# Filler matmuls, projections of rows not yet normed, and the recurrence's preparation woven into attention

## What is computed

```python
u = rmsnorm(h, attn_norm_pre[l])
proj = u @ w_in[l]
o_fox = forgetting_attention(fh(fq), fh(fk), fh(fv), ff, fox_forget_bias[l])   # 8 heads of 64, causal softmax
o_rwkv = rwkv7_time_mix(p_rwkv, ...)    # 8 heads of 64, a recurrence over the tokens
mix = jnp.concatenate([o_fox, o_rwkv], axis=-1) @ w_out[l]

# rwkv7_time_mix:
p_prev = jnp.concatenate([jnp.zeros_like(p[:, :1]), p[:, :-1]], axis=1)
p = p + shift_mu * (p_prev - p)
w = -jax.nn.softplus(-(w0 + jnp.tanh(w_lat) @ w_up)) - 0.5
a = jax.nn.sigmoid(a0 + a_lat @ a_up)
g = jax.nn.sigmoid(g_lat) @ g_up
kk = kk / jnp.maximum(jnp.linalg.norm(kk, axis=-1, keepdims=True), 1e-12)
S_t = S diag(w_t) + (S a_t) b_t^T + v_t k_t^T ;  y_t = S_t r_t
```

## Time and profile before

| | us |
|---|---|
| median of 3 runs | 3685.21 |
| lowest, highest | 3672.19, 3711.24 |
| profiled execution, own time | 3717.66 |
| its span | 3715.6 |
| PE busy | 3496.1 (94%) |
| DVE busy | 1811.7 (49%) |
| ACT busy | 1259.8 (34%) |
| POOL busy | 809.1 (22%) |
| mean granted clock | 0.955 |

### The profile page before, as it was taken

The page is one execution under the profiler, slowest core; times in us unless marked ns, Lnnn a source line. Parts: engine busy times, 40 slices in busy tenths (PEclk is TensorE's granted clock), DMA queues, the critical chain, the costliest instruction groups (busy, mean ns, idle before and its releaser), DMA issues.

```text
span 3715.6 us, 47117 instructions
## 1 busy us (share of the span) xinstructions
PE 3496.1 (94%) x16820; PEld 2843.6 (77%) x16820; DVE 1811.7 (49%) x3443; ACT 1259.8 (34%) x1663; POOL 809.1 (22%) x336
## 2 busy tenths in 40 slices
PE   7995999799997889999899999999999899999998
PEld 5662897568785777888787888888888788888886
DVE  2554441343204554222312489998989254444443
ACT  2223210233224553333323343344444233332332
POOL 5430000234442333333444434400000000000000
PEclk9996985899998999999999999999999999999999
DMA  3110000122232122222222334445555655555642
GB/s 115 52 46 6 1 1 1 46 74 96 86 101 69 67 68 74 74 72 70 79 96 91 106 117 142 140 156 178 193 179 178 223 201 187 186 193 206 204 147 75
DMA packets 145965, 408.07 MB, mean 110 GB/s; under 512 B 11176, under 2 KB 43944, under 8 KB 143536
## 3 DMA queue, kind: packets, MB, share of 16 engines
q1 hardware_dynamic: 73472, 265.85, 22.3%
q10 hardware_dynamic: 72368, 140.68, 10.5%
HBM read 337.28 MB, written 69.21 MB: 109 GB/s over the span
## 4 chain that ended last, share of the span: by engine, by line
PE 82%; DVE 13%; ACT 2%; issue 1%; ACTq 0%; DMA 0%; DVEq 0%
PE bank L322 22%; PE bank L324 21%; PE bank L323 21%; PE bank L823 2%; PE bank L345 1%; PE bank L821 1%; ACT arena L864 1%; DVE arena L1606 1%; PE bank L515 1%; PE bank L529 1%; PE bank L757 1%; PE bank L562 1%; DVE arena L1735 1%; PE bank L519 1%; PE bank L399 1%
## 5 line engine op out<-in xcount | busy, mean ns | idle before, releaser
L322 PE MATMUL bank<-xs,ring_hi 128*128 128x512 f32 x2488 | 999.9, 402 | 59.1 <-DVE xs L1338 44.4
L324 PE MATMUL bank<-xs,ring_lo 128*128 128x512 f32 x2488 | 977.1, 393 | 0.0
L323 PE MATMUL bank<-xs,ring_hi 128*128 128x512 f32 x2488 | 976.2, 392 | 0.0
L1310 POOL TENSOR_TENSOR ring_lo<-ring,ring_hi 128x1024 fp32r<-128x1024 f32 x262 | 650.6, 2486 | 1059.5 <-ACT ring_hi L864 1059.5
L864 ACT ACTIVATE arena<-bank 128x512 f32<-128x512 f32 (+6 forms) x639 | 424.6, 693 | 1243.6 <-PE bank L324 818.1
L864 ACT ACTIVATE ring_hi<-ring 128x1024 fp32r<-128x1024 f32 x468 | 494.7, 1059 | 500.4 <-DMA ring<-weights 238.8
L322 PEld LDWEIGHTS bank<-xs,ring_hi 128*128 128x128 f32 x2488 | 471.5, 189 | 171.9 <-issue 50.0
L324 PEld LDWEIGHTS bank<-xs,ring_lo 128*128 128x128 f32 x2488 | 471.2, 189 | 101.9
L323 PEld LDWEIGHTS bank<-xs,ring_hi 128*128 128x128 f32 x2488 | 472.4, 190 | 96.8 <-issue 3.5
L1748 DVE TENSOR_TENSOR ring_lo<-ring,ring_hi 128x1024 fp32r<-128x1024 f32 x206 | 252.2, 1224 | 383.9 <-ACT ring_hi L864 383.6
L322 PE MATMUL bank<-gw,ring_hi 128*128 128x512 f32 x1024 | 398.5, 389 | 0.7 <-ACT arena L864 0.7
(11 more groups left out here) (265 smaller groups left out, 4065.4 us busy)
## 6 DMA issues: line engine op xcount, KB each, us to landing
ring<-weights SPq DMA_DIRECT2D x503, 512.0 KB, 3.3
hidden<-arena ACTq DMA_DIRECT2D x128, 256.0 KB, 3.9
gates<-arena ACTq DMA_DIRECT2D x16, 2048.0 KB, 6.6
arena<-hidden ACTq DMA_DIRECT2D x16, 2048.0 KB, 10.4
arena<-gates ACTq DMA_DIRECT2D x16, 2048.0 KB, 17.2
xres<-x_t ACTq DMA_DIRECT2D x4, 512.0 KB, 7.2
out_t<-arena SPq DMA_DIRECT2D x1, 2048.0 KB, 7.1
arena<-ret_decay ACTq DMA_DIRECT2D x1, 1024.0 KB, 5.5
```

Of the source, the lines that this page charges most:

```text
L322: pe.matmul(out_, wh, x[0], start=start, stop=False, skip_group_check=True)
L323: pe.matmul(out_, wh, x[1], start=False, stop=False, skip_group_check=True)
L324: return pe.matmul(out_, wl, x[0], start=False, stop=stop, skip_group_check=True)
L1310: pool.tensor_tensor(ring_lo[:, r, :], ring[:, r, :], ring_hi[:, r, :].bitcast(F32), ALU.subtract).then_inc(lo_done, 1)
```

## The change

- **Rows not yet normed.** The input is scaled by the norm's weight alone and split at once; the first block is split by ACT and DVE instead of POOL. The sums of squares stand on PE behind block 0. The reciprocal root is multiplied in when DVE takes each product out of its bank (`normed`), in all 27 blocks, where ACT copied before. The weight loads start when half of the input has landed, and the constants are loaded after the input.
- **Order.** The first two recurrence blocks and the low-rank products now come ahead of attention. The other 12 blocks are done in units 0 to 11, four quarters a unit. The rest of the preparation is spread over units 12 to 30 (`rw_prepare`, on PE, DVE and ACT), behind each unit's own work.
- **Fillers.** `keep_clock` issues matmuls of a weight block with itself, of 512 columns, into a bank that nobody reads: 4 - t at two places in each of units 12 to 31 (100), 4 ahead of the scan, one a chunk, 2 behind the scan, and one for each head of the output.

The diff, cut to its core:

```diff
--- before.py
+++ after.py
-            sp.wait_ge(in_x[2], 16)
+            sp.wait_ge(in_x[1], 16)
...
+            def keep_clock(b, count):
+
+                r = B_WOUT % RING
+                for _ in range(count):
+                    pe.matmul(bank[b][:, :], ring_hi[:, r, 0:P], ring_hi[:, r, 0:T], start=True, stop=True, skip_group_check=True)
...
-            pe.wait_ge(in_cst, 16)
-            norm_sums(0, KD)
...
             for n in range(N_FOX):
                 product(n, [(n, KD)], XS, chunk_wait=xs_chunks(0) if n == 0 else None)
+                if n == 0:
+                    pe.wait_ge(in_cst, 16)
+                    norm_sums(0, KD)
+            for n in (N_FOX, N_FOX + 1):
+                pe.wait_ge(evac, n - 1)
+                ready(n)
+                for k in range(KD):
+                    mm = three(bank[n % 2][:, :], n, k, XS[k], k == 0, k == KD - 1)
+                mm.then_inc(block_used, 1)
...
+            su = arena[:, SMALL:SMALL + 3, :]
+            pe.wait_ge(in_small, 32)
+            pe.wait_ge(evac, N_FOX + 2)
+            for m in range(NPAIR):
+                cols = slice(m * P, (m + 1) * P)
+                pe.wait_ge(rw_act, 2 if m == 0 else 1 + 3 * m)
+                pe.matmul(bank[0][:, :], su[0:64, 0, cols], tile(LAT)[0:64, :], start=True, stop=True).then_inc(rw_pe, 1)
+                if m:
+                    pe.wait_ge(rw_act, 2 + 3 * m)
+                pe.matmul(bank[1][:, :], su[64:128, 0, cols], tile(LAT)[64:128, :], start=True, stop=True).then_inc(rw_pe, 1)
+                pe.wait_ge(rw_act, 3 + 3 * m)
+                pe.matmul(bank[2][:, :], su[:, 1, cols], tile(GL), start=True, stop=False)
+                pe.matmul(bank[2][:, :], su[0:32, 2, cols], tile(GFT)[0:32, :], start=False, stop=True).then_inc(rw_pe, 1)
...
-                if u < 2 * N_RW:
-                    rw_quarter(2 * u)
+                if u == 0:
+                    pe.wait_ge(rw_act, 15)
+                if u < N_RW - 2:
+                    rw_quarter(4 * u)
+                    rw_quarter(4 * u + 1)
+                if u == N_RW - 2:
+                    ready(B_WOUT)
+                if u >= N_RW - 2:
+                    if u % 8 == 0:
+                        pe.wait_ge(fo_out, m)
+                    keep_clock(2 + (m + 1) % 2, 4 - t)
                 pe.wait_ge(fnorm, u + 1)
...
-                if u < 2 * N_RW:
-                    rw_quarter(2 * u + 1)
+                if u < N_RW - 2:
+                    rw_quarter(4 * u + 2)
+                    rw_quarter(4 * u + 3)
+                if u >= N_RW - 2:
+                    keep_clock(2 + (m + 1) % 2, 4 - t)
...
+            def rw_prepare(u):
+
+                if u == 13:
+                    for m in range(NPAIR):
+                        pe.wait_ge(rw_act, 15 + m + 1)
+                        head_sums(1, m, tile(DT4[m])).then_inc(rw_pe, 1)
+                m = (u - 15) // 4
+                if u in (15, 19, 23, 27):
+                    pe.wait_ge(rw_inv, 1)
+                    if m:
+                        pe.wait_ge(rw_dve, 2 * m - 1)
+                    spread(RT4, m, 0).then_inc(rw_inv_out, 1)
+                if u in (17, 21, 25, 29):
+                    pe.wait_ge(rw_dve, 2 * m + 1)
+                    pe.matmul(bank[1][:, :], cc("bones"), tile(RKR), start=True, stop=True).then_inc(rw_pe, 1)
             fox_scores(0)
             for u in range(len(units)):
                 if u + 1 < len(units):
                     fox_scores(u + 1)
                 fox_out(u)
...
+                rw_prepare(u)
...
+            ready(B_WOUT)
+            keep_clock(7, 4)
             pe.wait_ge(rw_act, base_act)
             pe.wait_ge(rw_dve, base_dve)
             for c in range(NCH):
+                keep_clock(4, 1)
...
+            keep_clock(4, 2)
             pe.wait_ge(rw_dve, bd)
             for h in range(8):
+                keep_clock(6, 1)
...
-            act.dma_start(cst[:, :], cst_d).then_inc(in_cst, 16)
             for i in range(4):
                 act.dma_start(xres[:, 2 * i:2 * i + 2, :], xt.rearrange("(k p) t -> p k t", p=P)[:, 2 * i:2 * i + 2, :]
                               ).then_inc(in_x[i], 16)
+            act.dma_start(cst[:, :], cst_d).then_inc(in_cst, 16)
...
-            norm_squares(0, xr, lambda k: act.wait_ge(in_x[k // 2], 16))
-            norm_hi(0, 0)
...
+            for k in range(KD):
+                act.wait_ge(in_x[k // 2], 16)
+                A(XS[k][0], xr(k), ACT.Copy, scale=pp("attn_pre", k)).then_inc(hi_ready, 1)
+            act.wait_ge(loaded[0], 16)
+            A(ring_hi[:, 0, :], ring[:, 0, :], ACT.Copy).then_inc(first_hi, 1)
+            for k in range(KD):
+                norm_square(0, k, xr)
+            norm_root(0)
...
+            act.wait_ge(shifted, 2)
+            A(tile(GFT)[0:32, :], tile(GFT)[0:32, :], ACT.Sigmoid).then_inc(rw_act, 1)
+            A(tile(LAT)[0:64, :], tile(LAT)[0:64, :], ACT.Tanh).then_inc(rw_act, 1)
...
+            act.wait_ge(shifted, 3)
+            A(tile(GL), tile(GL), ACT.Sigmoid).then_inc(rw_act, 1)
...
+            def rw_prepare(u):
+
+                if u == 12:
+                    act.wait_ge(shifted, 11)
+                    for m in range(NPAIR):
+                        A(tile(DT4[m]), tile(RK + m), ACT.Square, scale=pp("k_k", m)).then_inc(rw_act, 1)
+                if u == 13:
+                    act.wait_ge(rw_pe, 16)
+                    A(roots[:, 0, :], bank[1][:, 0:TT * 8], ACT.Sqrt).then_inc(rw_act, 1)
+                if u in (14, 20, 24, 28):
+                    m = (u - 14) // 4
+                    if m:
+                        act.wait_ge(rw_dve, 2 * m)
+                    act.wait_ge(cum_ready, m + 1)
+                    st.go(A(tile(EL[4]), tile(EL[1]), ACT.Exp, scale=-E_HALF))
+                    st.go(A(tile(EL[5]), tile(EL[1]), ACT.Exp, scale=E_HALF))
+                    st.go(A(tile(EL[6]), tile(EL[2]), ACT.Exp, scale=-E_HALF))
+                    A(dch[:, 0, m * NCH:(m + 1) * NCH], ch(tile(EL[3]))[:, :, MID], ACT.Exp, scale=-E_HALF).then_inc(exp_ready, 1)
...
+            pool.sem_inc(split_hi, 1)
+            for r in range(1, RING):
+                split(r, r, 0, split_hi, w_split, r)
...
-            for x in in_x:
-                ve.wait_ge(x, 16)
             ve.wait_ge(in_par, 16)
+            for k in range(KD):
+                ve.wait_ge(hi_ready, k + 1)
+                STT(XS[k][1], xr(k), pp("attn_pre", k), XS[k][0].bitcast(F32), ALU.mult, ALU.subtract).then_inc(xs_ready, 1)
+            ve.wait_ge(first_hi, 1)
+            TTN(ring_lo[:, 0, :], ring[:, 0, :], ring_hi[:, 0, :].bitcast(F32), ALU.subtract).then_inc(w_split, 1)
             ve.wait_ge(in_cst, 16)
-            norm_scale(0, "attn_pre", 0, 0)
+            norm_root(0)
+
+            def normed(n, out_, b):
+
+                ve.wait_ge(block_used, n + 1)
+                TTN(out_, b[:, :], tile(NORM[0][1]), ALU.mult).then_inc(evac, 1)
...
+                normed(n, raw, bank[n % NBANK if n < N_FOX else n % 2])
...
+            shift(N_FOX, 1)
+            shift(N_FOX + 1, 2)
...
+            def rw_prepare(u):
+
+                if 1 <= u <= N_RW - 2:
+                    shift(N_FOX + 1 + u, 2 + u)
+                if u == 14:
+                    ve.wait_ge(rw_act, 20)
+                    st(TSM(roots[:, 0, :], roots[:, 0, :], 1e-12, None, ALU.max))
+                    inverse_roots(RT4)
+                if u in (13, 19, 23, 27):
+                    m = (u - 13) // 4
+                    if m:
+                        ve.wait_ge(exp_ready, m)
+                    st(ve.tensor_tensor_scan(tile(EL[3]), cc("reset"), tile(LW + m), 0.0, ALU.mult, ALU.add))
+                    cu = ch(tile(EL[3]))
+                    st(TTN(ch(tile(EL[1])), cu, cu[:, :, MID:MID + 1].to_broadcast([P, NCH, C]), ALU.subtract))
+                    TTN(tile(EL[2]), tile(EL[1]), tile(LW + m), ALU.subtract).then_inc(cum_ready, 1)
+                m = (u - 16) // 4
+                if not 0 <= m < NPAIR:
+                    return
+                R, K, V, kk, a = tile(RR + m), tile(RK + m), tile(RV + m), tile(KKT + m), tile(RA + m)
+                if u % 4 == 0:
+                    ve.wait_ge(rw_inv_out, m + 1)
+                    st.go(STT(kk, K, pp("k_k", m), bank[0][:, :], ALU.mult, ALU.mult))
+                    st(TSM(tile(EL[7]), a, 1.0, pp("k_a", m), ALU.subtract, ALU.mult))
+                    st(STT(K, tile(EL[7]), 1.0, K, ALU.add, ALU.mult))
+                    STT(tile(RKR), R, pp("r_k", m), K, ALU.mult, ALU.mult).then_inc(rw_dve, 1)
+                if u % 4 == 1:
+                    ve.wait_ge(rw_dve, 2 * m + 1)
+                    ve.wait_ge(exp_ready, m + 1)
+                    st.go(STT(tile(TA + m), kk, -1.0, tile(EL[6]), ALU.mult, ALU.mult))
+                    st.go(TTN(tile(TR + m), R, tile(EL[4]), ALU.mult))
+                    st(TTN(tile(TK + m), K, tile(EL[5]), ALU.mult))
+                if u % 4 == 2:
```

(5 more changed lines are left out.)

192 lines of the change are left out of this document (62 added, 130 removed).

## The result

| | before | after |
|---|---|---|
| median of 7 runs of each, on one chip | 3707.89 (3672.19 to 3723.50) | 3665.16 (3656.00 to 3669.43) |
| ratio, 95% interval | | 0.9887 (0.9849 to 0.9925) |
| profiled execution, own time | 3717.66 | 3656.49 |
| its span and granted clock | 3715.6, 0.955 | 3654.7, 0.974 |

The change makes the kernel faster, by 43 us in the medians and by 61 us in the two profiled executions. The forecast was 54. The time lies inside the range, but 34 us above the forecast time of 3631: by 23 us because the kernel before has a median of 3708 here and had one of 3685 in the three runs shown with it, and by 11 us because the gain in the medians is 43 and not 54.

What follows compares the result with a forecast made beforehand. PE was taken as the bound except in the start and preparation, bound by chains of waits. Gains of 6 ahead of the inversion, 22 in scan and 26 in output gave 54: 3685 - 54 = 3631 us, range 3600 to 3690.

Steps and rivals of the forecast that it cites:

- the likeliest case: Scan and output both hold the full clock: 3631 us, own range 3596 to 3660, chance 49 in 100.
- I apply the difference to the median: 3685 - 54 = 3631: Final step: the 54 us gain worked out on the profiled execution (3717.66) is subtracted from the median of 3685.
- 134 us, the least certain term: Attention units 12 to 31: 116.5 us for five heads at half full, half half clock, plus added work; inversion from 368.
- The extras: Added work in units 12 to 31: sums by head 5.5 us, products by pair 6.4, spreads 2.6, ACT's root 3.
- Start: Up to the thirteenth product: 12 us gained, first product at 15.5 instead of 31.37, thirteenth done at 96.6 instead of 108.4.
- the stated two thirds at 0.43 and the others at 0.225: Block 0 at the start: its 24 matmuls begin at half clock, taken as 8.3 us.
- chunk 3.95: Scan at full clock: 3.95 us a chunk with its filler instead of 7.00; stage 30.2 instead of 52.7, 22 gained.
- half of that, with 8 fillers of 0.225, is 27.5: Output stage at full clock: 51.3 us halved plus fillers, a gain of 24, or 26 with the product behind it.
- Falls in the output: Rival: clock holds in the scan but falls in the output; gain 25 us, time 3660, chance 27 in 100.
- Holds in neither: Rival: clock holds in neither scan nor output, fillers only lengthen both; time 3688, chance 13 in 100.
- Preparation does not fit: Rival: DVE's preparation adds to units 12 to 31, 16 units growing by 2.6 us; time 3756, chance 4 in 100.
- Issue-bound small products: Rival: the scan's 64 x 64 products are bound by issue whatever the clock; chunk 5.4, time 3641, chance 7 in 100.

Runs made afterwards that it cites:

- the bunched kernel: The changed kernel with the recurrence's preparation from unit 13 (PE, ACT) or 14 (DVE) on moved behind the last unit; 3695.36 us, ratio 0.9995 to before.
- the fitted ones: The changed kernel, only entry fillers kept in scan and output, attention fillers raised to (4, 5, 6, 4) and (4, 3, 2, 2); 3634.34 us, ratio 0.9828.

## Why the prediction was right or wrong

**The direction and the mechanism were right.** Both stages hold the full clock, which was the likeliest case, and this is where the gain comes from: 40.5 of the 60.9 us of the profiled pair, 48 forecast. The fillers at the entry do it; those in each chunk and head, on which the prediction also counted, are not needed. The sum is nearer than its terms: 54 for 60.9 is made of 11.6 us too little ahead of the inversion, 5.8 of chance in the inversion, 7.5 too much in scan and output, and 3 lost in the rest.

**The level was wrong, by the step "I apply the difference to the median: 3685 - 54 = 3631".** Of those three runs two, at 3672 and 3685, are of the fastest group; the median of 68 runs is 3711. The forecast saw that the profiled execution was 32 us slower and did not ask why. Scan and output at half clock cost 44 us (104.8 to 60.6 us), and the middles of the fastest and the slowest group lie 43 us apart (3673 and 3715), as if the fastest executions kept the clock there by chance. The clock of the stages in the trace, and the 39 us between three runs, were both in view. A difference worked out on an execution in the lower clock holds for executions like it only: 3717.66 - 54 = 3664 was the better forecast. It meets the median of 3665.16 partly by the errors above, which cancel.

**Late units, "134 us, the least certain term": 125.5.** The guess that the clock would be half full and half at half was right (0.77). The extras were nearly right: 7.0 for the sums, about 4 for the spreads and 4.6 for the products by pair. The 3 us of ACT around its root were not seen; in their place PE waits 2.48 us for DVE ahead of the sums, behind the shift of the last block's rows. Heads without these come to 22 us, not 23.3. With attention beginning at 130.35 and the last quarters done at 230.8, close to the forecast (130 and 233), this is the 17.6 instead of 6. That the start of attention met the forecast is partly luck: the other traces with the same code up to there have it from 127.5 to 135.9.

**Start: right in the sum.** First product 16.8 (15.5), the thirteenth done 96.4 (96.6). The later first product is made up by block 0, 7.1 us (8.3 forecast; the stated two thirds at 0.43 and the others at 0.225 would be 8.7), and by the sums, 6.9 (8). Of the 12 us, 7 are PE's wait for the root, and the others lie almost all in block 0, which the prediction did not price before the change.

**Scan, "chunk 3.95": 4.34, and 19.0 gained instead of 22.** The scan without fillers takes 30.3, and the forecast with them was 30.2. Two terms were mis-sized: the filler, about 0.42 a piece between narrow products instead of 0.225, and the other pieces of a chunk, 3.9 together and not 3.7.

**Output, "half of that, with 8 fillers of 0.225, is 27.5": 33.3.** A step of two L638, two L640 and four L644 takes 0.95 us; before, the same took 622.01 - 620.35 = 1.66. The ratio is 1.75, not 2. So the term that was mis-sized is the halving: the 51.3 us at half clock became 30.3 without fillers, not 25.7. The eight fillers add 3.0, not 1.8.

**The rivals.** "Falls in the output" is not what the changed kernel does, and its reason, too few fillers among narrow products, does not stand: both stages hold with none among them. But the clock fell there in the traced execution of the kernel with no filler in scan and output. "Holds in neither" falls. "Preparation does not fit" falls with the bunched kernel: 30 to 35 us are hidden. "Issue-bound small products" falls: 32 of L619 and L621 take 1.13 us in the chunk above, 35 ns each, where they took 61. The Trainium skill, page "TensorE: Matmul & The Clock Gate", section "Wait — 56ns, not 53.3ns?", gives about 62 ns a matmul for the sequencer's own code, and only with hardware decoding off. The prediction took the figure without that condition; the 35 ns measured here are below it, so it does not bind these products. The same page of the Trainium skill says in Part 4 that the full clock does not engage for transposes. Before the change, the clock was at 0.50 during the 16 transposes of L450 (335.61, 3.68 us, behind a wait of 2.15) and at 1.00 from 340 us on, right behind them, which speaks against it; the late units, a mixture with transposes, sat at 0.97 once enough wide fillers stood between, and at 0.55 without.

**What part of the change gives what.** By medians: entry fillers 35 (in the kernel before) or 42 (in the changed one), interleaving 30 to 35, attention fillers 4 to 13, PE's wait for the root about 4 to 8. The fillers in each chunk and head cost 8 to 13. That is more than 43 to 48 in all. The likely reason, which no run tests alone, is that the move also takes the quarters of the projections out of 16 units. They had covered waits and held the clock there; the fillers put that back only in part, and the fitted ones put back some 18 more.

## What to carry to other kernels

Before a difference is subtracted from a median, look at whether the runs have one level, and in which of its states the trace was taken; a stage at half clock with PE busy throughout is a candidate for a second level. Here two stages of dense, narrow matmuls sat at either clock for nearly their whole length, so look at the entry of such a stage: by the times the clock fell there in most executions, at a cost of up to 44 us, and four wide matmuls in the gap of half a microsecond ahead of it kept it. The gap alone is not enough for the fall, as one trace passed it at full clock. Put fillers into waits that the trace shows, as many as fit, and not among products that run without a gap, where each cost 0.4 us here and gave nothing.

## What was not expected of the hardware

The same 240 matmuls of the output stage, with PE busy for 98 to 99% of it in each case, took 52.0 us at a granted clock of 0.50 and 30.3 at 1.00, and neither level changed behind the first microsecond of the stage. The scan likewise took 51.4 us with PE busy in 51.31 of them, at half from less than 2 us behind its start to its end, and 30.3 at full. Sixteen wide matmuls, 6.2 us in all, raised it. A wide matmul costs 0.23 us in a row of its like and about 0.42 alone between products of 64 rows or columns.
